# Retention heads on centred V between gate chunks, chunk pairs that leave the last tile for the end, and a new place for the small tiles of the two hybrid layers

## What is computed

```python
def hybrid_layer(x, norm_g, w_in, w_br_a, w_br_b, w_br_c, w_out, cos, sin):
    h = rmsnorm(x, norm_g)
    proj = h @ w_in                      # q, k, v, gates of all branches
    ...
    return x + merged @ w_out

def ret_output(y, g, w_out):
    b, h, n, dv = y.shape
    yf = y.astype(jnp.float32)
    mu = jnp.mean(yf, axis=-1, keepdims=True)
    var = jnp.mean(jnp.square(yf - mu), axis=-1, keepdims=True)
    yn = ((yf - mu) * lax.rsqrt(var + NORM_EPS)).astype(g.dtype)
    yn = yn.transpose(0, 2, 1, 3).reshape(b, n, h * dv)
    return (jax.nn.silu(g) * yn) @ w_out
```

## Time and profile before

| | us |
|---|---|
| median of 3 runs | 2439.43 |
| lowest and highest run | 2438.74, 2444.33 |
| the profiled execution | 2442.71 |
| its span in the trace | 2440.5 |
| PE busy | 2326.1 (95%) |
| POOL, DVE, ACT busy | 1355.8, 1156.3, 816.6 |
| weights and tables moved | 356.25 MB, mean 146 GB/s |

### The profile page before, as it was taken

The page is one execution under the profiler, slowest core; times in us unless marked ns, Lnnn a source line. Parts: engine busy times, 40 slices in busy tenths (PEclk is TensorE's granted clock), DMA queues, the critical chain, the costliest instruction groups (busy, mean ns, idle before and its releaser), DMA issues.

```text
span 2440.5 us, 39512 instructions
## 1 busy us (share of the span) xinstructions
PE 2326.1 (95%) x13560; PEld 2036.2 (83%) x13560; DVE 1156.3 (47%) x2158; ACT 816.6 (33%) x1166; POOL 1355.8 (56%) x714
## 2 busy tenths in 40 slices
PE   7999989899999999999999999999999999778997
PEld 6988989889888888778888888888889789568997
DVE  6653477553765552356655324655325210564233
ACT  4354443544432221303222223222213215214653
POOL 6754778637755554403655543655445447037996
PEclk9999999999999999999999999999999999888999
DMA  7842458524365543302655333655334324014554
GB/s 253 275 131 78 136 197 280 176 81 131 121 216 199 182 146 97 125 9 87 232 182 204 109 95 107 223 189 202 113 91 142 106 96 149 15 35 139 182 171 137
DMA packets 112985, 356.25 MB, mean 146 GB/s; under 512 B 13184, under 2 KB 22912, under 8 KB 112640
## 3 DMA queue, kind: packets, MB, share of 16 engines
q1 hardware_dynamic: 112896, 355.05, 44.9%
HBM read 347.40 MB, written 1.05 MB: 143 GB/s over the span
## 4 chain that ended last, share of the span: by engine, by line
PE 79%; issue 9%; DVE 6%; POOL 4%; ACT 1%; SPq 1%; DMA 1%; DVEq 0%; POOLq 0%; ACTq 0%
PE ps L1768 22%; PE ps L1769 22%; PE ps L1770 22%; POOL w_low L937 3%; PE ps L1876 2%; PE ps L1796 1%; PE ps L1798 1%; PE ps L1797 1%; PE ps L1894 1%; PE ps L1884 1%; PE ps L1927 1%; PE ps L2223 1%; PE ps L2224 1%; PE ps L2225 1%; PE ps L2185 1%
## 5 line engine op out<-in xcount | busy, mean ns | idle before, releaser
L937 POOL TENSOR_TENSOR w_low<-raw,w_high 128x1024 fp32r<-128x1024 f32 (+3 forms) x544 | 1207.0, 2226 | 705.5 <-ACT w_high L539 704.5
L1768 PE MATMUL ps<-h_high,w_high 128*128 128x256 f32 (+1 forms) x2784 | 919.6, 330 | 40.6 <-DVE h_low L1089 18.1
L539 ACT ACTIVATE w_high<-raw 128x1024 fp32r<-128x1024 f32 (+3 forms) x544 | 536.7, 988 | 1205.0 <-PE ps L1770 950.4
L1769 PE MATMUL ps<-h_low,w_high 128*128 128x256 f32 (+1 forms) x2784 | 909.3, 327 | 0.0
L1770 PE MATMUL ps<-h_high,w_low 128*128 128x256 f32 (+1 forms) x2784 | 909.2, 327 | 0.0
L1768 PEld LDWEIGHTS ps<-h_high,w_high 128*128 128x128 f32 x2784 | 535.6, 192 | 90.4 <-issue 23.5
L1769 PEld LDWEIGHTS ps<-h_low,w_high 128*128 128x128 f32 x2784 | 535.7, 192 | 42.6
L1770 PEld LDWEIGHTS ps<-h_high,w_low 128*128 128x128 f32 x2784 | 534.9, 192 | 42.8
L1768 PE MATMUL ps<-act_high,w_high 128*128 128x512 f32 (+1 forms) x770 | 267.7, 348 | 0.0
L1769 PE MATMUL ps<-act_low,w_high 128*128 128x512 f32 (+1 forms) x770 | 267.1, 347 | 0.0
L1770 PE MATMUL ps<-act_high,w_low 128*128 128x512 f32 (+1 forms) x770 | 267.1, 347 | 0.0
(11 more groups left out here) (206 smaller groups left out, 2290.5 us busy)
## 6 DMA issues: line engine op xcount, KB each, us to landing
raw<-in_w_dram SPq DMA_DIRECT2D x216, 512.0 KB, 3.6
raw<-in_wu_dram SPq DMA_DIRECT2D x176, 512.0 KB, 4.5
ada<-in_ada_dram SPq DMA_DIRECT2D x144, 512.0 KB, 4.1
raw<-in_wd_dram SPq DMA_DIRECT2D x64, 384.0 KB, 3.1
raw<-in_wd_dram SPq DMA_DIRECT2D x64, 320.0 KB, 2.9
raw<-in_wv_dram SPq DMA_DIRECT2D x24, 408.0 KB, 4.7
heads<-rot SPq DMA_DIRECT2D x96, 64.0 KB, 3.4
ada<-in_cond_dram SPq DMA_DIRECT2D x6, 512.0 KB, 4.9
```

The lines of the kernel that those rows point to most:

```text
L539: e.activation(wh[:, c % RING, 0:width], raw[:, c % RING, 0:width], ACT.Copy).then_inc(hi_done, 1)
L937: e.tensor_tensor(wl[:, c % RING, 0:width], raw[:, c % RING, 0:width], wh[:, c % RING, 0:width].bitcast(F32), ALU.subtract).then_inc(lo_do ...
L1768: e.matmul(ps[:, bank, to:to + n], wh[:, j, w], hi, start=(first and t == tiles[0]), stop=False)
L1769: e.matmul(ps[:, bank, to:to + n], wh[:, j, w], low, start=False, stop=False)
```

## The change

1. **Start of the run.** DVE makes the low parts of weight chunks 0 and 1 (`first_low`), POOL starts with chunk 2. ACT makes the squares of x, DVE adds them in PSUM, PE adds the last two parts. The table for the root is loaded after the third split.
2. **Chunk pairs (`duo`).** The first two chunks of `qk` and of `out` run as a pair: tiles 0 to 6 of chunk 0, tiles 0 to 6 of chunk 1, then tile 7 of both. The sums of squares follow the pair. `out` gets a bank for nearly each chunk (OUT_BANKS, OUT_FREE).
3. **Between the layers.** The new x of `out` is formed in its PSUM bank (`out_summed`); ACT makes high part, square and copy from there, DVE the low part from PSUM, and the squares are summed in PSUM. The root of the q/k norm is kept in PSUM as well, with a copy in SBUF (`rs_kept`, for which the second SiLU waits); the roots follow chunk 0 and the SiLU chunk 1.
4. **Scaled tiles.** DVE forms them after the first value group (g == 0) instead of the third (VG - 2 = 2); ACT's high parts stand between the splits of chunks 7 to 10 of `vn` (TILES_FROM) instead of behind all of them.
5. **Trios.** The second trio of `up0`, `up1` and `up2` is taken chunk by chunk.
6. **rv.** The banks of the groups change places (`rv_bank`); ACT copies the values out of PSUM with scale -1/512 and sums them by token (`vmean`), DVE rescales and adds that mean, which centres V.
7. **Heads.** No mean of y is formed. The gate chunks of `rg` stand among the parts of the heads, in banks 6 and 7; ACT makes their SiLU, the squares of y, the root and the high parts; DVE multiplies y by the gate before the norm's factor is there. Between two gate chunks POOL makes the low parts. The first four `ro` chunks are cut so that tiles of heads 0 to 2 come before those of head 3. The mask is in the distances now (fp32, 1 MB instead of 0.5 MB, with a very large distance where the mask was 0), `dmask` goes.

The core of the diff (eight to twelve leading spaces left out):

```diff
-OUT_BANKS = (3, 0, 1, 2)
+OUT_BANKS = (3, 6, 0, 1, 2, 3, 6, 2)
+OUT_FREE = (0, 3, 4, 4, 4, 5, 6, 9)
+TILES_FROM = 2 * RING - 1
...
 split(0, 0, 0, CW)
-table_for_sqrt()
 for k in range(KT):
     if k % 2 == 0:
         e.wait_ge(x_in[k // 2], 16)
     plain_high(0, k)
-    if k == 3:
-        split(0, 1, 1, CW)
+split(0, 1, 1, CW)
+first_squares = ps[:, 4:6, :].rearrange("p a (b t) -> p (a b) t", b=2)
+e.activation(first_squares, x[:, 0, 0:4, :], ACT.Square).then_inc(x_squared, 1)
+e.activation(nb[:, 0:2, :].rearrange("p a (b t) -> p (a b) t", b=2), x[:, 0, 4:8, :], ACT.Square)\
+    .then_inc(x_squared, 1)
 split(0, 2, 2, CW)
+table_for_sqrt()
...
-        if c >= VN + AHEAD - 4:
-            for k in (2 * (c - VN - AHEAD + 4), 2 * (c - VN - AHEAD + 4) + 1):
+        if 0 <= c - TILES_FROM < KT // 2:
+            for k in (2 * (c - TILES_FROM), 2 * (c - TILES_FROM) + 1):
...
-            e.wait_ge(emptied_d, 4 + d0 + k + 1)
-            plain_high(L + 1, k)
+            new = ps[:, OUT_BANKS[k], 0:T]
+            e.wait_ge(out_summed, k + 1)
+            e.activation(hh[:, k, T:2 * T], new, ACT.Copy, scale=col("norm_g", (L + 1) * KT + k))\
+                .then_inc(norm_hi, 1)
+            if k >= 2:
+                e.wait_ge(out_added, k - 1)
+            e.activation(sq[:, 1, T * (k % 2):T * (k % 2) + T], new, ACT.Square).then_inc(out_squared, 1)
+            e.activation(xk(k, 1)[:, 0, :], new, ACT.Copy).then_inc(x_copied, 1)
...
+    e.wait_ge(chunk_done, 1 + later["rv"][0] + k + 1)
+    for tt in range(2 * TT):
+        e.activation(vr[:, tt, RDV * g:RDV * g + RDV], ps[:, rv_bank(g) + tt, :], ACT.Copy, scale=-1.0 / RDV,
+                     accum_out=vmean[:, tt, g:g + 1]).then_inc(rv_out, 1)
...
+for c in range(4):
+    next_split(c)
+    gate_silu(c)
 for h in range(RH):
-    if h + 1 < RH:
+    next_split(4 * h + 4)
+    head_squares(h)
+    if h < RH - 1:
         decays(h + 1)
-
-    e.wait_ge(rc_done, 4 * h + 4)
-    e.activation(rs[:, 0:T], ps[:, 7, 0:T], ACT.Sqrt, bias=eps[:, :], scale=1.0 / RDV)\
-        .then_inc(rstd, 1)
-phase(later["ro"], W8, W8)
+        gate_silu(4 * h + 4)
+        next_split(4 * h + 5)
+        gate_silu(4 * h + 5)
+    else:
+        table_for_sqrt()
+    head_root(h)
+    if h < RH - 1:
+        next_split(4 * h + 6)
+    head_high(h)
+    if h < RH - 1:
+        gate_silu(4 * h + 6)
+        next_split(4 * h + 7)
+        gate_silu(4 * h + 7)
...
+for c in range(4 * RH):
+    if c % 4 == 3 and c > 3:
+        head_low(c // 4 - 1)
+    split(m_rg + c + AHEAD, c + AHEAD, CW)
+split(later["ro"][0] + AHEAD, AHEAD, CW)
+head_low(RH - 1)
...
+first_low(0)
 for k in range(KT):
-    if k % 2 == 0:
-        e.wait_ge(x_in[k // 2], 16)
     plain_low(0, k)
-squares = nb[:, :, :].rearrange("p a (b t) -> p (a b) t", b=2)
-for k in (0, 4):
-    e.tensor_tensor(squares[:, k:k + 4, :], x[:, 0, k:k + 4, :], x[:, 0, k:k + 4, :], ALU.mult)\
-        .then_inc(dve_step, 1)
+first_low(1)
+e.wait_ge(x_squared, 2)
...
-        if g == VG - 2:
+        if g == 0:
...
-        e.tensor_tensor(squares, xs, xs, ALU.mult).then_inc(dve_step, 1)
-        plain_low(L + 1, k)
...
+        new = ps[:, OUT_BANKS[k], 0:T]
+        e.scalar_tensor_tensor(out=new, in0=new, scalar=0.25, in1=xk(k, 1)[:, 0, :], op0=ALU.mult,
+                               op1=ALU.add).then_inc(out_summed, 1)
+        e.wait_ge(norm_hi, 4 * KT * (L + 1) + k + 1)
+        e.wait_ge(x_copied, k + 1)
+        e.scalar_tensor_tensor(out=hl[:, k, T:2 * T], in0=new, scalar=col("norm_g", (L + 1) * KT + k),
+                               in1=hh[:, k, T:2 * T].bitcast(F32), op0=ALU.mult, op1=ALU.subtract)\
+            .then_inc(norm_split, 1)
...
+        here = vr[:, tt, RDV * g:RDV * g + RDV]
+        e.wait_ge(rv_out, 4 * g + tt + 1)
+        e.tensor_scalar(here, here, -1.0 * RDV, vmean[:, tt, g:g + 1], ALU.mult, ALU.add)\
+            .then_inc(emptied_d, 1)
...
-        e.tensor_tensor(dec[:, b, 0:2, :], dec[:, b, 0:2, :], dmask[:, b, :, :], ALU.mult)\
...
+        e.wait_ge(emptied_a, 4 + a0 + 4 * h + dv + 1)
+        e.wait_ge(ry_squared, 4 * h + dv + 1)
+        e.tensor_tensor(yr[:, dv, :], ps[:, 2 + dv, 0:T], sgr[:, 4 * h + dv, :], ALU.mult).then_inc(ry_out, 1)
...
+    e.wait_ge(rstd, h + 1)
+    e.reciprocal(ps[:, 0, 0:T], ps[:, 0, 0:T]).then_inc(dve_step, 1)
...
-        e.tensor_tensor(yr[:, dv, :], yr[:, dv, :], sq[:, 0, T:2 * T], ALU.subtract).then_inc(dve_step, 1)
...
+        e.tensor_tensor(yr[:, dv, :], yr[:, dv, :], ps[:, 0, 0:T], ALU.mult).then_inc(r_scaled, 1)
...
+def duo(m0, banks, lo, free, ready):
+
+    for n, (c, k) in enumerate([(0, k) for k in range(KT - 1)] + [(1, k) for k in range(KT - 1)]
+                               + [(0, KT - 1), (1, KT - 1)]):
+        if k == 0:
+            e.wait_ge(lo_done, RING + m0 + c + 1)
+            free(c)
+        if c == 0:
+            ready(k)
+        end = one(banks[c], c, k, k, lo, T, k == 0, k == KT - 1, h, 0)
+        if k == KT - 1:
+            end.then_inc(chunk_done, 1)
...
-chunk_trio(m0, 0, n_split.now + 4 + KT, True, after_out, nothing, None)
+chunk_trio(m0, 0, n_split.now + 4 + KT, True, after_out, nothing, None, True)
...
-        natural(c, c, RDV, 4 * (g % 2), 2 * TT, c == 0, c == 3).then_inc(chunk_done, 1)
-e.wait_ge(emptied_d, 4 + d0 + 12)
-plain(later["rg"], T, emptied_a)
-e.wait_ge(emptied_d, 4 + later["ro"][1])
-e.wait_ge(emptied_a, 4 + later["ro"][2])
-
-def scores(h_):
-    for jt in range(4):
+        if c == 0 and g == 1:
+            e.wait_ge(emptied_d, 4 + d0)
+        if c == 0 and g > 1:
+            e.wait_ge(rv_out, 4 * g - 4)
...
+    products(6 + c % 2, c % RING, range(KT), 0, h, 0, T, True, True).then_inc(chunk_done, 1)
...
-        end = e.matmul(ps[:, 6, 0:T], ones[:, :], yr[:, dv, :], start=(dv == 0), stop=(dv == 3))
-    end.then_inc(rmean, 1)
...
+gate_chunk(0)
+gate_chunk(1)
+e.wait_ge(rv_out, 16)
+scores(0, range(4))
+gate_chunk(2)
+gate_chunk(3)
+e.wait_ge(emptied_d, 4 + d0 + 16)
+for h_ in range(RH - 1):
+    values(h_)
+    gate_chunk(4 * h_ + 4)
+    scores(h_ + 1, (0, 1))
+    gate_chunk(4 * h_ + 5)
+    scores(h_ + 1, (2, 3))
+    variance(h_)
+    gate_chunk(4 * h_ + 6)
+    gate_chunk(4 * h_ + 7)
+values(RH - 1)
...
+gated_products(0, range(KT), True).then_inc(chunk_done, 1)
+variance(RH - 1)
+e.wait_ge(lo_done, RING + m0 + 2)
+gated_products(1, range(KT, 12), True)
+e.wait_ge(lo_done, RING + m0 + 3)
+gated_products(2, range(KT))
+e.wait_ge(lo_done, RING + m0 + 4)
+gated_products(3, range(KT, 12))
+gated_products(1, range(12, 16), True).then_inc(chunk_done, 2)
+gated_products(3, range(12, 16)).then_inc(chunk_done, 1)
```

More of the change, by code:

```diff
@@ L966, in norm_low @@
                             .then_inc(norm_split, 1)
-            for c in range(AHEAD):
-                split(c, c, CW)
+            e.wait_ge(lo_done, RING + 2)
+            split(2, 2, CW)
             for L in range(LAYERS):
@@ L1685, in _ @@
             decayed_scores(0)
+            a0 = later["rg"][2]
             for h in range(RH):
@@ L1959, in _ @@
                 n_split(KT)
-                plain(of_layer("out", L), T, emptied_d, ready=tile_ready, banks=OUT_BANKS)
-            n_act, n_tailsq = Tally(), Tally()
-            def one(bank, j, t, k, lo, n, first, last, m=h):
-                w = slice(t * P, t * P + P)
-                out, hi, low = ps[:, bank, lo:lo + n], m[0][:, k, lo:lo + n], m[1][:, k, lo:lo + n]
-                e.matmul(out, wh[:, j, w], hi, start=first, stop=False)
-                e.matmul(out, wh[:, j, w], low, start=False, stop=False)
-                return e.matmul(out, wl[:, j, w], hi, start=False, stop=last)
+                m0, d0, _, _ = of_layer("out", L)
+                duo(m0, OUT_BANKS, 0, lambda c: e.wait_ge(emptied_d, d0 + OUT_FREE[c]), tile_ready)
+                for k in range(2, OUT):
+                    e.wait_ge(lo_done, RING + m0 + k + 1)
+                    e.wait_ge(emptied_d, d0 + OUT_FREE[k])
+                    products(OUT_BANKS[k], k % RING, range(KT), 0, h, 0, T, True, True).then_inc(chunk_done, 1)
+            n_act, n_tailsq = Tally(), Tally()
             def totals_of_tail(bank, q, *last):
@@ new lines, in _, with gated_products @@
+            values(RH - 1)
+            m0, d0, a0, n = later["ro"]
+            def gated_products(j, fs, ready=False):
+                for f in fs:
+                    if ready:
+                        e.wait_ge(rgn, f + 1)
+                    w = slice(f % KT * P, f % KT * P + P)
+                    (mh, ml), out = gated_tile(f), ps[:, 6 + j // 2, 0:T]
+                    e.matmul(out, wh[:, j, w], mh, start=(f == 0), stop=False)
+                    e.matmul(out, wh[:, j, w], ml, start=False, stop=False)
+                    end = e.matmul(out, wl[:, j, w], mh, start=False, stop=(f == 2 * KT - 1))
+                return end
```

298 lines of the change are left out of this document (166 added, 132 removed).

## The result

The changed kernel takes 2349.5 us (median of 4 runs, 2348.0 to 2351.2), the kernel before 2440.7 us beside it: ratio 0.962, 95% interval 0.961 to 0.964, 3.8% faster. Forecast were 2350 us and 92.8 us of gain; the profiled executions differ by 94.7 us (2442.7 to 2348.0).

A forecast was written before the change was run, and what follows sets the result against it. PE, busy 95% of the span, was taken to bound the kernel. Terms of 54, 6.4, 8, 9.4, 4, 12 and -1 gave 92.8 us off 2442.7, so 2349.9; forecast 2350 (2335 to 2360), eight in ten 2334 to 2384.

The forecast's parts named there:

- Half clock: After PE's waits, products run at clock 0.51; a 6.9 us stretch at that clock was priced as 3.4 us lost.
- Retention: First gate chunk to last output chunk: 141.7 us if PE never waits, against 199.5 before; 54 us gain, ends 36 to 58.
- 8.7 us of slack a head: Retention heads: ACT's work of 15.2 us fits a 23.9 us head step, the argument against ACT's order binding.
- the rival: Retention heads: ACT's single queue makes PE wait 3 us in each of four heads; about 2369 us, up to 2385; chance 0.19.
- rv, 6.4: Start of rv: with other banks for the first group PE no longer waits for rotated k tiles; 6.4 us, 3.5 to 6.7.
- Start, 8: First-layer start: input tiles' low halves come earlier, then the load behind the SiLU decides; 8 us, 5.7 to 10.3.
- Output to q/k: Output of layer 0 into layer 1: last-tile and input-tile waits and their half clock go; 9.4 us, 6 to 11.7.
- output of layer 1: Last-tile wait before the first output chunk, 2.5 us covered and 1.7 of half clock; 4 us, 2.5 to 4.5.
- Scaled tiles: Index products of both layers: tiles made earlier, 9.7 us per layer vanish, less charges for late splits; 12 us, 4 to 17.
- Trios: Second trio of up0, up1, up2 by chunk: first chunk may wait for last tiles; -1 us, from -3 to +1.
- Slower side: Heads: the four-slot ring stops running ahead, each of 16 gate chunks waits 8.5 us for its weights; 2486 us, chance 0.02.
- doesn't do what it says: Heads: gaps stay, only mean products and covered gate waits go, some 12 of 54 us; 2392 us, chance 0.04.

The follow-up runs named there:

- the second trace: The changed kernel, unedited, run and traced once more beside the other follow-up runs: 2349.2 us, ratio 0.9624 against the kernel before.

## Why the prediction was right, and where its steps were not

- **Bound and method.** PE sets the time, and gains are idle PE and half clock. Held: 94.7 us between the profiled runs. In the spans, 94.3 us apart, the seven named places give 97.5, and 3.2 us went where the forecast had nothing: the square of the last output tile (-1.7) and all else (-1.5).
- **Half clock.** The forecast charged half of every such stretch. But where PE also stands idle in it, that time is in the wait already: the earlier trace rows has PE busy in 4.27 of the 6.90 us from 123.8 us, which costs 2.1 and not 3.4 us. At the index products the charge was too high by 1.3 us in the first layer and 0.9 in the second.
- **Retention, 54 forecast, 59.4 measured.** The mechanism held, with no waits at all in the heads. The size lies above the best end that was given, 58: the allowance of 4 us for waits was not needed, and a 128x256 fp32 product takes 0.42 us in a row of them instead of 0.44. The 7.07 us in the earlier trace rows hold the tail of the last one; in the changed kernel values that start at 2006.47 are followed by the next product at 2013.19, 6.72 us for 16. With 0.42 the sum of 141.7 becomes 139.2, and PE took 140.1. The heads hold 13 table loads, not 11 (6 before).
- **ACT's room.** The step "8.7 us of slack a head" was wrong as an argument. The work of 15.2 us is about right (14.8 to 15.9 us of ACT in a step of 23.6), but the rival hung on the nearest due time, which is 1.7 us away. ACT's order was much nearer to binding than this reason says. By the 2.7 us that the Trainium skill (ScalarE: Activation LUTs, "Rules for kernel authors") budgets for a table switch, the load ahead of the decays would have used 1.4 of the 1.7 us, by estimate. The trace shows 1.28 us again for every load.
- **rv, 6.4 and 6.3.** Right in both parts: 3.7 us by the first value chunk (forecast 3.5), and 2.6 behind it (2.9). This part was read from the traces and never taken back alone.
- **Start, 8 and 8.8.** Size right, cause half wrong. The weight load behind the SiLU was to set chunk 6 at 33.1 us (29.2 and 3.5 give 32.7; the 33.1 has 0.4 us that no figure in it explains, and so has the like time of layer 1). PE reached it at 32.1, held not by the load but by DVE, which had a conditioning row's product ahead of the rotation: with that order turned round PE was there at 30.9. And what POOL's work costs DVE here was overrated: POOL making these splits costs nothing that can be measured.
- **Output to q/k, 9.4 and 8.5; output of layer 1, 4 and 3.9.** Right, the second by both the trace and the run without pairs. What wasn't seen is that 1.7 us of the second go straight away to the square of the last tile. The first was read from the traces, where chunk 6 of layer 1 starts at 337.6 us, 353.5 with the 15.9 us gained ahead of it (forecast 353).
- **Scaled tiles, 12 and 13.9.** Two errors cancel in part. The old loss is about 8.4 us a layer and not 9.7, for the reason under half clock. The 2 us a layer charged for late splits were 0.3 and 0.2, with the ReLU's 0.9 and 0.4 beside them, and no half clock followed. Taken back alone the part is worth 16.
- **Trios, -1 and -3.3.** Outside its bounds of -3 to +1 in the first trace, inside them in the second (-2.3). The mis-sized step is what the chunk 4 wait gives back: I let it absorb the loss, but it is tied to a load that waits for a signal of its own, so it absorbs 1.5 to 1.8 us. The losses were 2.1, 3.8 and 2.5, the second with 1.3 us of half clock that the second trace does not have.
- **Slower side and "doesn't do what it says".** Nothing of either was seen: the ring ran ahead through the heads, and PE waited for no low part of a weight there.

## What to carry to other kernels

Holes of a latency chain are best filled with work that needs another resource; here 16 weight chunks among the heads gave 22 us, and the shorter chain with its fewer products about 37. An engine's mean idle time did not tell its room: look for the result with the nearest due time, and try it by repeating one operation. When you price a wait, count the half clock only where the engine is busy in it, or the same time is counted twice. A queue that waits for one consumer's signal delays everything behind it, so put loads that don't need the signal ahead of the wait; and a wait that follows a fixed-time event gives or takes back part of any gain ahead of it.
